# Passages between stages turned and multiplied by token tile, and a first FFN unit that uses the accumulator banks

## The reference, cut to what matters

```python
D_MODEL, SEQ, DEPTH, D_FF = 1024, 256, 2, 2816
def rms_norm(x):     return x * rsqrt(mean(x * x, -1) + 1e-6)
def modulate(x, shift, scale): return rms_norm(x) * (1 + scale) + shift
def swiglu(u, w_gate, w_up, w_down): return (silu(u @ w_gate) * (u @ w_up)) @ w_down

for l in range(DEPTH):
    sh1, sc1, g1, sh2, sc2, g2, sh3, sc3, g3 = split(silu(c) @ w_ada[l] + b_ada[l], 9)
    x = x + 0.5 * g1 * swiglu(modulate(x, sh1, sc1), ffn1_gate[l], ffn1_up[l], ffn1_down[l])
    x = x + g2 * token_mix(modulate(x, sh2, sc2), w_in[l], ..., w_out[l])    # two attentions, merged
    x = x + 0.5 * g3 * swiglu(modulate(x, sh3, sc3), ffn2_gate[l], ffn2_up[l], ffn2_down[l])
x = rms_norm(x) * final_norm
# hybrid layer, once
x = x + gate1 * (merge(conv(h), attention(h)) @ w_o)       # h = modulate(x, shift1, scale1)
x = x + gate2 * moe(modulate(x, shift2, scale2))           # 32 experts, 2 of one group per token
```

## Time and profile before

| | |
|---|---|
| time, median of three runs | 1783.75 us (1783.61 to 1784.79) |
| the profiled execution | span 1780.2 us; the runs' median is 3.55 us above it |
| PE busy | 1722.7 us, 97% of the span |
| DVE busy | 1366.2 us, 77% |
| ACT busy | 967.8 us, 54% |
| DMA | 437.45 MB, mean 246 GB/s |

### The profile page before, as it was taken

One profiled execution on the slowest core, in us unless ns is written; L12 is line 12 of the kernel. 1 busy time (PEld: TensorE's weight loads), 2 busy tenths in 40 slices (PEclk: granted clock), 3 DMA queues, 4 the chain that ended last, 5 costly groups with the idle time before them and its releaser, 6 DMA issues.

```text
span 1780.2 us, 25032 instructions
## 1 busy us (share of the span) xinstructions
PE 1722.7 (97%) x8696; PEld 1403.6 (79%) x8696; DVE 1366.2 (77%) x2067; ACT 967.8 (54%) x1472; POOL 47.0 (3%) x92
## 2 busy tenths in 40 slices
PE   6999998999999999999989999999999998999998
PEld 3878787887788878887878877888787876888886
DVE  7887777757776578777687678876768479999997
ACT  5444463755544454445546655444535647777775
POOL 0000000000000000000000000000000000000000
PEclk9999999999999999999999999999999999999999
DMA  8998853234677748886623348987473444999994
GB/s 348 353 358 325 316 212 108 96 113 172 235 284 259 260 164 326 326 304 251 237 85 106 119 165 294 350 308 278 169 295 118 184 165 168 380 341 366 374 355 165
DMA packets 61803, 437.45 MB, mean 246 GB/s; under 512 B 6816, under 2 KB 7328, under 8 KB 9504
## 3 DMA queue, kind: packets, MB, share of 16 engines
q1 hardware_dynamic: 47360, 338.44, 50.8%
q0 software_dynamic: 12672, 92.28, 13.9%
q10 hardware_dynamic: 1696, 5.72, 0.9%
HBM read 435.36 MB, written 1.05 MB: 245 GB/s over the span
## 4 chain that ended last, share of the span: by engine, by line
PE 82%; DVE 10%; ACT 4%; DMA 2%; issue 2%; SPq 0%; DVEq 0%; ACTq 0%; POOLq 0%
PE bank L1910 24%; PE bank L1911 24%; PE bank L1912 24%; DVE w_lo L999 3%; PE bank L2160 2%; DVE ada_w L1031 2%; PE bank L2178 1%; DMA arena<-ada_pairs 1%; ACT w_hi L522 1%; PE bank L1900 1%; PE bank L2004 1%; DMA ada_w<-ada_pairs 1%; PE bank L2140 1%; PE bank L2134 1%; PE bank L2138 0%
## 5 line engine op out<-in xcount | busy, mean ns | idle before, releaser
L999 DVE TENSOR_TENSOR w_lo<-raw,w_hi 128x1024 fp32r<-128x1024 f32 x426 | 501.7, 1221 | 163.0 <-ACT w_hi L522 162.0
L522 ACT ACTIVATE w_hi<-raw 128x1024 fp32r<-128x1024 f32 x426 | 426.6, 1052 | 329.5 <-PE bank L1912 319.2
L1910 PE MATMUL bank<-w_hi,uT_hi 128*128 128x512 f32 (+2 forms) x1408 | 550.4, 391 | 16.3 <-DVE uT_lo L1390 7.1
L1911 PE MATMUL bank<-w_lo,uT_hi 128*128 128x512 f32 (+2 forms) x1408 | 537.3, 382 | 0.0
L1912 PE MATMUL bank<-w_hi,uT_lo 128*128 128x512 f32 (+2 forms) x1408 | 536.8, 381 | 0.0
L1910 PEld LDWEIGHTS bank<-w_hi,uT_hi 128*128 128x128 f32 x1408 | 266.4, 189 | 74.9 <-DVE uT_lo L1390 9.1
L1912 PEld LDWEIGHTS bank<-w_hi,uT_lo 128*128 128x128 f32 x1408 | 265.7, 189 | 51.9
L1911 PEld LDWEIGHTS bank<-w_lo,uT_hi 128*128 128x128 f32 x1408 | 266.5, 189 | 46.5
L1910 PE MATMUL bank<-w_hi,r_arena 128*128 128x512 f32 (+1 forms) x744 | 293.5, 394 | 5.4 <-DVE r_arena L1808 2.5
L1912 PE MATMUL bank<-w_hi,r_arena 128*128 128x512 f32 (+1 forms) x744 | 288.8, 388 | 0.0
L1911 PE MATMUL bank<-w_lo,r_arena 128*128 128x512 f32 (+1 forms) x744 | 288.5, 388 | 0.0
(11 more groups left out here) (339 smaller groups left out, 1479.0 us busy)
## 6 DMA issues: line engine op xcount, KB each, us to landing
raw<-weight_stream SPq DMA_DIRECT2D x216, 1024.0 KB, 5.2
ada_w<-ada_pairs POOLq DMA_DIRECT2D x88, 1024.0 KB, 5.6
raw<-expert_blocks SPq DMA_DIRECT2D x48, 1024.0 KB, 4.9
ada_w<-expert_blocks SPq DMA_DIRECT2D x32, 1024.0 KB, 4.9
cmpw<-expert_blocks SPq DMA_DIRECT2D x16, 1024.0 KB, 5.1
arena<-ada_pairs SPq DMA_DIRECT2D x5, 1024.0 KB, 13.4
ada_w<-ada_pairs SPq DMA_DIRECT2D x3, 1024.0 KB, 13.4
cmpw<-compress_w ACTq DMA_DIRECT2D x2, 1024.0 KB, 7.4
```

The lines of the kernel that those rows point to most:

```text
L522: act.activation(w_hi[:, b], v, ACT.Copy).then_inc(hi_done, 1)
L999: V.tensor_tensor(w_lo[:, b], v, f32(w_hi[:, b]), ALU.subtract).then_inc(split_done, 1)
L1910: pe.matmul(dst, xh, w_hi[:, off:off + n], start=first, stop=False, skip_group_check=True)
L1911: pe.matmul(dst, xh, w_lo[:, off:off + n], start=False, stop=False, skip_group_check=True)
```

## The change

**Passages A, C, D** (`norm_behind_ffn`). ACT, and not DVE, scales t0's x. PE runs fewer fillers (6 or 7), turns t0 alone, and starts the products of t0; t1's transposes stand ahead of t0's fifth k-tile (k4). The columns of the first unit go tile by tile: eight k-tiles of t0, then eight of t1 (`first_columns`; `gate_up_behind` in C). Shift, rounding and remainder are made for one token tile at a time, so there are twice as many, of half the size. On DVE the norm of t1 and the splits of the unit's second block stand between the remainders of t0.

**Passages B, E** (`norm_behind_merge`). t0 is turned inside the merge's last product group. In B the first FFN unit's products go t0 k0 to k3, t1 k0 to k3, then both again with k4 to k7; its first block is loaded into the slot of the merge's last unit that had none (`early`). In E the gates and 12 fillers stand ahead of t1's transposes.

**FFN.** The first unit's gate and up go to ACC banks 0 and 1, and `down` of that unit starts the accumulators (`first=True`), so the four zero matmuls go. The gate transposes of A move behind the first unit's columns (first half) and the second unit's (second half). The transposes of x go to banks 4 to 7 (`XT`).

```diff
@@ ACT
-            def norm(q, n, late=None, c_row=None, behind_ffn=False, between=lambda: None):
...
+            def scale(q, t):
+                act.wait_ge(rstd_done, 2 * q + t + 1)
+                for h in range(2):
+                    c = slice(h * 512, (h + 1) * 512)
+                    act.activation(xn[:, t, c], x[:, t, c], ACT.Copy, scale=rstd[:, t:t + 1]).then_inc(xn_done, 1)
...
+            def norm_behind_ffn(q, n, between=lambda: None):
+                squares(q, 0)
                 root(q, 0)
+                scale(q, 0)
+                rounded_u(n, 0, (0, 1))
+                square(q, 1, 0)
+                rounded_u(n, 0, (2, 3))
                 square(q, 1, 1)
                 root(q, 1)
...
+                between()
+                rounded_u(n, 1, (0, 1))
+                rounded_u(n, 1, (2, 3))
@@ DVE
+            def norm_behind_ffn(q, n, late):
+
+                shifted(n, 0)
+                remainder(n, 0, (0,))
+                rms_sum(q, 1)
+                remainder(n, 0, (1,))
+                rms_inverse(q, 1)
+                rms_scale(q, 1)
+                remainder(n, 0, (2,))
+                split_half(late, 1, 0)
+                remainder(n, 0, (3,))
+                split_half(late, 1, 1)
+                shifted(n, 1)
+                remainder(n, 1, range(4))
+
+            def norm_behind_merge(stage, q, n, done, between):
+
+                for h in range(2):
+                    x_half(stage, 0, h, done)
+                norm_tile(q, 0)
+                x_half(stage, 1, 0, done)
+                shifted(n, 0)
+                remainder(n, 0, (0, 1))
+                x_half(stage, 1, 1, done)
+                remainder(n, 0, (2, 3))
+                between(0)
+                norm_tile(q, 1)
+                shifted(n, 1)
+                remainder(n, 1, (0, 1))
+                between(1)
+                remainder(n, 1, (2, 3))
@@ PE
-            def norm(n, q):
-                keep_warm(16, GU[0][:, :])
...
+            def restart(n, q, warm):
+                pe.wait_ge(x_ready, 4 * q + 1)
+                keep_warm(warm, ACC[0][:, :])
+                turn_x(n, q, 0)
...
+            def first_columns(u, n, q):
+
+                seen, m = set(), None
+                for t in range(T):
+                    for k in range(KD):
+                        off = k * 768
+                        if (t, k) == (0, 4):
+                            turn_x(n, q, 1)
+                        need(u, seen, off, 768)
+                        if k % 2 == 0:
+                            pe.wait_ge(uT_ready, 8 * n + 4 * t + k // 2 + 1)
...
@@ PE, FFN
-                if nn > 0:
-                    pe.wait_ge(mod_ready, nn + 4)
-                    keep_warm(12, GU[0][:, :])
-                    gate_up(u0, nn, BY_K_TILE)
-                for b in range(4):
-
-                    pe.matmul(ACC[b][:, :], zeros[:, 0:P], zeros[:, :], start=True, stop=False, skip_group_check=True)
-                pe.wait_ge(h_done, 2 * f0 + 1)
                 gate_up(u0 + 1, order=BY_TILE_K, at_={(0, 1): lambda: turn(f0)})
-                down(u0, f0)
+                down(u0, f0, first=True)
@@ PE, main program
-                norm(l * 3 + 1, l * 3 + 1)
-                for h, b in enumerate((HT, GU[1])):
-                    gate(l * 3 + 1, h, b)
...
+                restart(l * 3 + 1, l * 3 + 1, 6)
+                first_columns(u_mix, l * 3 + 1, l * 3 + 1)
+                gate(l * 3 + 1, 0, HT)
+                columns(u_mix + 1, 768, 3)
+                pe.wait_ge(gate_ready, l * 6 + 3)
+                gate(l * 3 + 1, 1, HT)
```

More of the change, by code:

```diff
@@ L543, in root, with squares @@
                 act.activation(sq[:, t:t + 1], ms[:, t:t + 1], ACT.Sqrt, scale=1.0 / D, bias=eps).then_inc(sq_done, 1)
[L545 to L556, removed]
-                    square(q, t, h)
+            def squares(q, t):
+                for h in range(2):
+                    square(q, t, h)
@@ new lines, in norm_behind_ffn, with norm_behind_merge @@
+                between()
+                rounded_u(n, 1, (0, 1))
+                rounded_u(n, 1, (2, 3))
+            def norm_behind_merge(q, n, between, ahead=lambda: None):
+                squares(q, 0)
+                root(q, 0)
+                rounded_u(n, 0, (0, 1))
+                square(q, 1, 0)
+                rounded_u(n, 0, (2, 3))
+                between(0)
+                square(q, 1, 1)
+                root(q, 1)
+                between(1)
+                rounded_u(n, 1, (0, 1))
+                rounded_u(n, 1, (2, 3))
@@ L668, in _ @@
             sqrt_ahead(0)
-            rms_squares(0)
+            for t in range(T):
+                squares(0, t)
+                root(0, t)
             def first_hi(b):
@@ L795, in _ @@
             act.dma_start(fn_bc, fnorm).then_inc(c_landed, 16)
-            rms_squares_ffn(q6)
-            norm(q6 + 1, n6)
+            squares(q6, 0)
+            root(q6, 0)
+            squares(q6, 1)
+            root(q6, 1)
             u = HYB_U0
-            split(u, (2,))
+            norm_behind_ffn(q6 + 1, n6, lambda: split(u, (2,)))
             def split_f():
@@ L1057, in norm_tile, with split_half, behind_early @@
                 rms_scale(q, t)
-            def norm(q, n, tiles=range(T), late=None):
-                for t in tiles:
-                    norm_tile(q, t)
+            def split_half(u, j, i, skipped=0):
+                b, v = halves(j, raw[:, j * BLK:(j + 1) * BLK])[i]
+                dve.wait_ge(hi_done, (u * 3 + j) * HALVES + i + 1)
+                V.tensor_tensor(w_lo[:, b], v, f32(w_hi[:, b]), ALU.subtract).then_inc(split_done, 1 + skipped)
+            def behind_early(u, i):
+                split_half(u, 1, i, 0 if i else HALVES)
@@ L1079, in norm, with remainder @@
-                remainder(1)
-                remainder(2)
-                remainder(3)
-                if late is not None:
-                    split(late, (1,))
-            def hidden(f, tiles=range(T)):
+            def remainder(n, t, bs):
+                for b in bs:
+                    pair = slice(2 * b, 2 * b + 2)
+                    dve.wait_ge(uT_hi_done, 8 * n + 4 * t + b + 1)
+                    V.tensor_tensor(uT_lo[:, pair, tok(t)], uTf[:, pair, tok(t)], f32(uT_hi[:, pair, tok(t)]),
+                                    ALU.subtract).then_inc(uT_ready, 1)
@@ L1266, in ffn2, with merge @@
                 last_unit(u0 + n - 1, f0 + n - 1)
-                x_update_ffn(stage, f0 + n - 1, (used[2], u0 + n + 1), last=l == DEPTH - 1)
-            def merge(u0, m, stage, gates, following, between, more=True):
+                x_update_ffn(stage, f0 + n - 1, (used[2], u0 + n + 1))
+            def merge(u0, m, stage, gates, following, q, n, between):
                 split(u0, (2,))
@@ L1594, in _ @@
             dve.wait_ge(x_ready, 4 * (q6 + 2))
-            norm(q6 + 1, n6, late=HYB_U0)
+            rms_sum(q6 + 1, 0)
+            rms_inverse(q6 + 1, 0)
+            norm_behind_ffn(q6 + 1, n6, HYB_U0)
             u = HYB_U0
@@ L2719 @@
     stream[places.reshape(-1)] = blocks[:MOE_U0 * 3]
+    for l in range(DEPTH):
+        u = l * LAYER_UNITS + FFN_UNITS + MIX_IN_UNITS + MERGE_UNITS
+        stream[3 * u - 1] = blocks[3 * u]
     w_ada = np.concatenate([a["w_ada"].reshape(DEPTH, D, 3, 3 * D).transpose(0, 2, 1, 3).reshape(-1, D, 3 * D),
```

283 lines of the change are left out of this document (152 added, 131 removed).

## The result

The changed kernel took 1806.78 us (median of four runs, 1806.52 to 1811.05) against 1783.68 us (four runs) for the kernel before: ratio 1.0137, 95% interval 1.012 to 1.0153. In a second set it was 1813.13 us against 1782.39, ratio 1.017 (1.0148 to 1.0193). The forecast was +15.9 us; it was +23.1 and +30.7. The first median lies at the upper edge of the range (1807), the ratio carried to 1783.75 us (1808.2) and the second set above it. The direction was right and the size too small. A run's device time stands 1.6 to 2.2 us above its span wherever both are listed (1811.05 and 1809.2 for the profiled execution). By that, some 1.4 to 1.9 of the 3.55 us that were laid to the launch are that the profiled execution before was faster than its set's median. The changed kernel's profiled execution was 4.3 us slower than its set's.

The account below looks back on a forecast made before the run. PE was taken as the bound, with 82% of the chain of waits. Work +12.9 and clock +3 on 1780.2, plus 3.55 for median less profiled span, gave 1799.7 us; range 1786 to 1807.

Parts of the forecast that it names:

- the 3.55 us that were laid to the launch: Whole kernel: median of the runs less the profiled span, added to the forecast total, 3.55 us.
- The clock: Behind six new stalls of 3.3 to 3.7 us: two taken to cost clock, +3 us; all would be 10.
- rival 4: Six new stalls: every one halves the clock behind it, 12.9 + 10, 1806.7 us; chance 12%.
- Passage A: Passage A, twice: start 3.2 us earlier, new stalls at k2 (+3.3) and k5 (+3.65) of t0; +5.1 us each.
- the term -0.94: Passage A: waits of 0.94 us, read as lying between the old products, go away.
- the gates: Passage A: their eight transposes lay in the gap, now four behind each of two units, +1.1 us.
- Passage B: Passage B, twice: earlier products less waits of 2.2 and 2.0 for t1, -1.85 each; -3.3 for both after 0.4 for DMA.
- D: Passage D, once: same order as A, start gains only 1.6 us, gates stay; +5.7 us.
- C: Passage C: products start earlier, but the first hidden tile waits behind DVE's modulation passes; -0.7 us (0 to -3).
- E: Passage E: later DVE addition and ACT rounding ahead of t1's last square, before the last router product; +1.3 us (-1 to +3).
- The first FFN: First FFN: zero matmuls and a wait go, 1.5 us, but a later wait for data leaves only -0.4 us.
- Rival 1: Passages A and D: DVE and ACT keep pace, no new stalls, A -2.0, D -1.4, total 1775 us; chance 8%.

Follow-up runs that it names:

- the filled one: Changed kernel with matmuls on zeros in PE's new waits of passages A, B, C and D, nothing else changed: 1797.48 us, ratio 1.0069.
- the three order experiments: Changed kernel with DVE's split halves moved earlier: second and third block 1783.78 us, only the second 1802.28 us, only the third 1793.43 us.
- The new order with fillers: Changed kernel with DVE's second and third block halves moved earlier and zero matmuls in the waits left: 1774.25 us, ratio 0.9934.
- the order experiment: Changed kernel with only DVE's order changed in A, C, D: second block's halves before t1's sum, third's (A, D) around t1's shifts: 1783.78 us.
- the faster version: Changed kernel with DVE's halves reordered, zero matmuls in remaining waits, and t1's norm ahead of the second block in B and E: 1772.50 us, again 1772.74.

## Why the prediction was wrong

**The clock** is the term that failed. The forecast took two falls of six stalls, +3. In the changed kernel's profile A lost 3.1 and 5.2 us to it, B 2.65 and 2.7 (each the changed kernel's stretch less the filled one's), D 1.4, the attention 1.6 in each layer: 18.3 us, of which the hybrid layer gave 3.4 back. That leaves 14.9 where the forecast had 3. The step that failed is the one that let only idle times near the 4.16 us of the earlier trace rows cost clock. It counted six stalls of 3.3 to 3.7 us and gave nothing to B, to the attention, or to the wait of 1.85 us before A's first product, which the forecast itself had (0.2 + 1.3 + 0.4). B's falls come behind waits of 1.90 and 1.76, and the long one in A of layer 1 behind that 1.85. Its rival 4, every stall halves the clock, gave 1806.7 us, the closest number; it counted A and D only, too much in D and nothing in B and the attention, so that its nearness is in part luck. Its chance was 12%.

**Passage A** was right: +5.1 forecast, +5.14 and +5.13 measured at full clock, from the start (1.85 us of wait before the first product; 1.9 worked out) through both stalls. Order alone makes them, by the three order experiments. That the sum agrees to 0.1 is luck: the 0.94 us of the earlier trace rows stand ahead of the first product, outside the 17.29 us, and not between the products. A pair takes 1.05 (starts at 231.04 and 232.09 in the kernel before), which leaves 0.5 between them, so the term -0.94 should have been -0.5; the gates then cost 0.8 and not 1.1.

**Passage B** was mis-sized the other way: -2.71 and not -1.85 each, and nothing had to be taken off for the DMA. The two waits for t1, 1.90 and 1.76 and not 2.2 and 2.0, make 0.5 of the 0.9; the rest is not traced. **D** was right too, though the ledger has +4.3 for it. PE of the changed kernel at D, first product, k2 and k5 of t0:

```profile
1287.35 0.77 PE L1960 MATMUL bank<-w_hi,uT_hi 128*128 128x512 f32 x1 [1.85 <-DVE uT_lo L1113]
...
1292.71 0.50 PE L1960 MATMUL bank<-w_hi,uT_hi 128*128 128x512 f32 x1 [1.70 <-DVE w_lo L1095]
...
1300.46 0.79 PE L1960 MATMUL bank<-w_hi,uT_hi 128*128 128x512 f32 x1 [3.46 <-DVE w_lo L1032]
```

The wait at k2 is only 1.70, but k2 starts 5.36 us behind the first product as in A: the two pairs ahead of it ran at the lower clock, so part of the wait was spent in them. From the FFN's last product to the unit's release D takes 7.7 us longer than before in the changed kernel, and 6.3 with fillers (forecast 5.7). The ledger's stretch also holds the hybrid layer, where the kernel before has 5.1 us of its clock missing and the changed one 1.7; that hides 3.4 us of it.

**C** (-0.72) and **E** (+1.09) were right. With the clock full the terms of the passages sum to 5.14 + 5.13 + 6.3 - 5.42 - 0.72 + 1.1 = +11.5, where the forecast had 10.3 + 5.7 - 3.3 - 0.7 + 1.3 = +13.3.

**The first FFN** was to bring -0.4 and moves between -0.51 and +3.24. The longer wait behind it is shown; that it varies with the state of the weight stream is only argued.

**Open:** what the other three runs of the first set (1806.5 to 1806.8) had in place of the profiled one's 1811.05; why the attention stretch loses 1.6 us in most variants and not in the one profile of the kernel before, with the same waits of 0.84 and 1.7 us in both; and what decides whether the clock falls behind a given wait, since the same 1.85 us before A's first product was followed by a fall at once in some layers and runs and not in others.

**Rival 1** (DVE and ACT keep pace, 1775 us) did not happen. The new order with fillers gives about its price, 1774.25 us, by other terms: A is -0.8 there and not the -2.0 of the rival, B -2.7 and not -1.65. The Trainium skill ("Perfetto Trace Analysis", Optimizing Scalar/DVE Operations) has it that smaller instructions can let work end sooner; the trace agrees for the first product (4.45 us behind the FFN and not 7.63), and shows what it costs where the pieces stand in the wrong order.

## What to carry to other kernels

When work is cut into smaller pieces so that a waiting engine starts sooner, walk the queue of the engine that feeds it past the first piece: a short instruction that waits for a third engine holds everything that is written behind it, and here a weight split behind one row sum cost 3 us. Price each new idle time of TensorE twice, once for itself and once for the clock that may fall behind it, short ones among products too, and fill it with matmuls on zeros where a bank is free. Take the sum of a stretch from a run in which the clock is full; otherwise order and clock can't be told apart.

## What the runs showed of the hardware

- The granted clock fell behind waits of 1.90 and 1.76 us with products between them (0.50 in the window behind), and did not behind one idle time of 3.07 us that transposes and gates followed. Behind the same wait of 1.85 us before A's first product it fell within 1.2 us in layer 0 of the order experiment and not in layer 1. In the changed kernel the falls in A, B and the attention came back at the same places in both profiled executions, and these stretches were as long to 0.13 us.
- A filled wait costs nothing by itself: 11 and 12 matmuls on zeros left k2's distance at 5.35 us against 5.37, and gave 1.5 us back before k5.
- Of the chip's clock 34.1 us were missing in the changed kernel and 5.9 in the best profile of the faster version.
